# Three instead of two seven-product pairs in the gate/up stage of a two-layer trunk, with its chunks written out as straight code

## The reference

```python
def swiglu_ffn(x, norm_g, w_gate, w_up, w_down):
    h = rms_norm(x, norm_g)
    return (jax.nn.silu(h @ w_gate) * (h @ w_up)) @ w_down
```

## Time and profile before

| | |
|---|---|
| median of 3 runs | 2124.43 us (2124.36 to 2124.97) |
| the profiled execution | 2123.94 us |
| its span | 2121.8 us |
| TensorE busy | 2110.1 us, 99% |
| VectorE busy | 1415.5 us, 67% |
| ScalarE busy | 1079.8 us, 51% |
| DMA queue of the loads | 56.5% of the 16 engines' span |
| HBM | 189 GB/s over the span |

### The profile page before, as it was taken

How to read it: one execution, slowest core, us unless ns; L and a number is a source line. 1 busy time by engine, 2 the same in 40 slices (tenths; PEclk the granted TensorE clock), 3 DMA queues, 4 the chain that set the end, 5 groups by cost and what they waited for, 6 DMA issues and landing times.

```text
span 2121.8 us, 25577 instructions
## 1 busy us (share of the span) xinstructions
PE 2110.1 (99%) x9638; PEld 1751.7 (83%) x9638; DVE 1415.5 (67%) x1553; ACT 1079.8 (51%) x1308; POOL 35.7 (2%) x47
## 2 busy tenths in 40 slices
PE   9999999999999999999999999999999999999999
PEld 7888878888888888888888888878888888888887
DVE  5466577775677578855556565577874677578754
ACT  6443555553444345545566565465553444355532
POOL 1000000000000000000000001000000000000000
PEclk9999999999999999999999999999999999999999
DMA  8655546555655556655555444546555655566653
GB/s 326 209 177 169 175 164 229 178 198 189 213 194 178 198 187 207 201 177 180 197 179 171 165 162 162 172 159 224 171 198 198 215 182 178 198 198 199 210 171 134
DMA packets 202625, 402.80 MB, mean 190 GB/s; under 512 B 7120, under 2 KB 7728, under 8 KB 202288
## 3 DMA queue, kind: packets, MB, share of 16 engines
q1 hardware_dynamic: 201760, 398.49, 56.5%
q0 software_dynamic: 784, 3.19, 0.4%
HBM read 399.56 MB, written 2.10 MB: 189 GB/s over the span
## 4 chain that ended last, share of the span: by engine, by line
PE 97%; DVE 2%; ACT 1%; DMA 0%; issue 0%; SPq 0%; ACTq 0%
PE acc L1252 17%; PE acc L1256 17%; PE acc L1254 17%; PE acc L1393 13%; PE acc L1395 13%; PE acc L1394 13%; PE tr L1300 2%; PE tr L1394 1%; PE tr L1393 1%; PE tr L1395 1%; DVE w_lo L830 0%; DMA raw<-in_a_w_in_dram 0%; DVE a_lo L856 0%; PE tr L1363 0%; PE tr L1515 0%; PE tr L1525 0%
## 5 line engine op out<-in xcount | busy, mean ns | idle before, releaser
L830 DVE TENSOR_TENSOR w_lo<-raw,w_hi 128x1024 fp32r<-128x1024 f32 x567 | 685.0, 1222 | 441.3 <-ACT w_hi L476 440.7
L476 ACT ACTIVATE w_hi<-raw 128x1024 fp32r<-128x1024 f32 x567 | 597.4, 1060 | 674.5 <-PE acc L1256 359.3
L1393 PE MATMUL acc<-w_hi,a_hi 128*128 128x512 f32 x1056 | 412.7, 391 | 3.4 <-DVE w_lo L830 3.4
L1395 PE MATMUL acc<-w_hi,a_lo 128*128 128x512 f32 x1056 | 411.1, 389 | 0.0
L1394 PE MATMUL acc<-w_lo,a_hi 128*128 128x512 f32 x1056 | 410.8, 389 | 0.0
L1252 PE MATMUL acc<-w_hi,h_hi 128*128 128x512 f32 x696 | 271.6, 390 | 0.0
L1256 PE MATMUL acc<-w_hi,h_lo 128*128 128x512 f32 x696 | 270.9, 389 | 0.0
L1254 PE MATMUL acc<-w_lo,h_hi 128*128 128x512 f32 x696 | 270.8, 389 | 0.0
L1252 PE MATMUL acc<-w_hi,a_hi 128*128 128x512 f32 x640 | 255.1, 399 | 0.8 <-DVE a_lo L856 0.5
L1256 PE MATMUL acc<-w_hi,a_lo 128*128 128x512 f32 x640 | 249.8, 390 | 0.0
L1254 PE MATMUL acc<-w_lo,a_hi 128*128 128x512 f32 x640 | 249.4, 390 | 0.0
(11 more groups left out here) (187 smaller groups left out, 2262.6 us busy)
## 6 DMA issues: line engine op xcount, KB each, us to landing
raw<-in_ffn_w_down_dram SPq DMA_DIRECT2D x88, 1024.0 KB, 5.1
raw<-in_ffn_w_gate_dram SPq DMA_DIRECT2D x66, 1024.0 KB, 5.1
raw<-in_ffn_w_up_dram SPq DMA_DIRECT2D x66, 1024.0 KB, 5.1
raw<-in_a_w_in_dram SPq DMA_DIRECT2D x30, 1024.0 KB, 5.5
raw<-in_ffn_w_gate_dram SPq DMA_DIRECT2D x44, 512.0 KB, 3.7
raw<-in_ffn_w_up_dram SPq DMA_DIRECT2D x44, 512.0 KB, 4.5
raw<-in_a_w_out_dram SPq DMA_DIRECT2D x16, 1024.0 KB, 5.1
raw<-in_w_v_dram SPq DMA_DIRECT2D x16, 1024.0 KB, 5.1
```

What stands on the lines that cost most here:

```text
L476: nc.scalar.activation(dst, src, ACT.Copy).then_inc(hi_split, 1)
L830: nc.vector.tensor_tensor(lo, src, hi, ALU.subtract).then_inc(lo_split, 1)
L1393: nc.tensor.matmul(bank[:, :], hi, rhs_hi, start=start, stop=False)
L1395: return nc.tensor.matmul(bank[:, :], lo, rhs_hi, start=False, stop=stop)
```

## The change

WINO becomes 3: half groups 0, 1 and 2 of gate and up are pairs. That holds for the 20 chunks that are not the first of a layer. The first chunk of a layer keeps two pairs and its order. The other chunks have ten half groups and three pairs, in this order (g is gate, u is up, s a pair): g3 g4 g5 g6 g7 u7 s0 u3 s1 u4 s2 u5 u6. The half group u7 now stands ahead of the first pair; between the pairs lies one half group each. The loads follow in an order of their own, with one load of half a gate and half an up pair of half groups (g7 u7). The forms cover three pairs, f_hi and f_lo grow by half, and the sums of the forms are in a buffer of their own, form_a. On VectorE, `pair_sums` of a pair stands after the half group that comes before the pair's own, or, for the pair 0 of a layer's first chunk, after u2 rather than after u3. The transposes of the chunk before move from behind the third half group to behind the second. The wait for `hidden_lo` moves from before pair 0 to before the products in pair 0 that write the banks tr. The loops over chunks become straight code on all engines, the half groups' slot in the ring goes by the running number, and the two semaphores of landed pairs are one for each slot. The work of a chunk's hooks is the same.

The diff, cut to its core (the loads, the down stage, the ScalarE side and the code that works out slots and counts follow the lists in the same way; the code removed on VectorE and SyncE is that of the functions above):

```diff
-    WINO = 2
-    PLAIN = 2 * (KB // HG - WINO)
...
+    WINO = 3
...
+    ORDER_1 = items("g2 g3 g4 g5 u2 u3 g6 s0 g7 u4 u5 s1 u6 u7")
+    LOADS_1 = [items(w) for w in ("g2 g3", "g4 g5", "u2 u3", "g6 g7", "s0", "u4 u5", "s1", "u6 u7")]
+    ORDER_N = items("g3 g4 g5 g6 g7 u7 s0 u3 s1 u4 s2 u5 u6")
+    LOADS_N = [items(w) for w in ("g3 g4", "g5 g6", "g7 u7", "s0", "u3 u4", "s1", "s2", "u5 u6")]
...
-    GU_ORDER = [(m, j) for m in range(2) for j in range(6)]
-    GU_WINO = {5: 0, 9: 1}
-    GU_RAW = (0, 1, 2, 0, 1, 3)
-    GU_WINO_RAW = (3, 2)
-    GU_ORDER_1 = [(0, 0), (0, 1), (0, 2), (0, 3), (1, 0), (1, 1), (0, 4), (0, 5), (1, 2), (1, 3), (1, 4), (1, 5)]
-    GU_WINO_1 = {6: 0, 9: 1}
-    GU_RAW_1 = (0, 1, 2, 3, 1, 3)
-    GU_WINO_RAW_1 = (0, 2)
...
+            form_a = sb("form_a", [P, WINO, CH], F32, part)
...
+            def slot_free(layer, n):
+                what, count = SLOT_READ[layer][n - RAW]
+                sp.wait_ge(s_split if what == "pair" else lo_split, count)
...
+            def forms(layer):
+                a = form_a
+                if layer:
+                    dve.wait_ge(s_used, 3 * (LAST_PAIR[layer - 1, NF - 1] + 1))
+                step.inc(nc.vector.tensor_tensor(a[:, :, :].rearrange("p a c -> p (a c)"),
                                                  a_hi[:, 0:2 * WINO, :].rearrange("p k s -> p (k s)").bitcast(F32),
                                                  a_lo[:, 0:2 * WINO, :].rearrange("p k s -> p (k s)").bitcast(F32), ALU.add))
-                a11, a21, a12, a22 = (sums_b[:, 0:2, n * P:(n + 1) * P] for n in range(4))
-                s1, s2, s3, s4 = (sums_b[:, 2:4, n * P:(n + 1) * P] for n in range(4))
+                a11, a21, a12, a22 = (a[:, :, n * P:(n + 1) * P] for n in range(4))
+                s1, s2, s3, s4 = (sums_b[:, 0:WINO, n * P:(n + 1) * P] for n in range(4))
...
+                        if c == 0:
+                            hooks = {("g", 2): [lambda: forms(layer)], ("g", 4): [lambda: forms_lo_part(layer)],
+                                     ("g", 5): [first_hooks[0][0]], ("u", 2): [lambda: sums(c, 0)],
+                                     ("u", 3): [first_hooks[0][1]], ("u", 4): [lambda: sums(c, 1)]}
+                        else:
+                            hooks = {("g", 6): [], ("u", 7): [lambda: sums(c, 0)], ("u", 3): [lambda: sums(c, 1)],
+                                     ("u", 4): [lambda: sums(c, 2)]}
+                            if c > c0:
+                                hooks[("g", 4)] = [lambda: gate_sums(c - 1)]
+                                hooks[("g", 5)] = [lambda: hidden(c - 1, CHUNK_END[layer, c - 1])]
+                                hooks[("g", 6)].insert(0, lambda: dve.wait_ge(staged, b0 + c - NC))
+                                hooks[("s", 0)] = [lambda: hidden_lo(c - 1, c0)]
+                            else:
+                                hooks[("g", 6)].insert(0, first_hooks[p][0])
...
+                if tr_read is not None:
+                    pe.wait_ge(lhs_lo, tr_read)
                 products(tr[0], form(s1), *t1, start=first, stop=last)
                 products(tr[1], form(s3), *t3, start=first, stop=last).then_inc(s_used, 1)
...
-                        for q, (matrix, j) in enumerate(order):
-                            if first_layer and (matrix, j) == (1, 0):
+                            pe.wait_ge(gate_ready, NF * layer + c)
+                        begun = set()
+                        for item in order(c):
+                            m, q = item
+                            if c == 0 and item == ("u", 2):
                                 pe.wait_ge(staged, b0 - NC)
-                            if first_layer and (matrix, j) == (0, 4):
+                            if c == 0 and item == ("g", 6):
                                 pe.wait_ge(lhs_lo, b0)
-                            begins = j == 0 and (matrix == 0 or first_layer)
-                            plain_group(hg + q, q, matrix, j, (begins, j == 0),
-                                        (matrix == 1 and j == 5, matrix == 1 and j == 5))
-                            if first_layer and q == 3:
+                            if item == ("s", 0) and c == 0:
+                                pe.wait_ge(forms_lo, layer + 1)
+                            if item == ("u", 7) and c:
+                                if c == c0:
+                                    pe.wait_ge(part_added, added)
+                                else:
+                                    pe.wait_ge(staged, b0 + c - NC)
+                            if m == "s":
+                                pair(PAIR_OF[layer, c, q], q, q == 0, q == pairs(c)[-1], "u" not in begun,
+                                     b0 + c if q == 0 else None)
+                                begun |= {"up 0"}
+                            else:
+                                s = "gu".index(m)
+                                if m == "u":
+                                    starts = "u" not in begun and "up 0" not in begun, "u" not in begun
+                                else:
+                                    starts = ("g" not in begun,) * 2
+                                plain_group(HG_OF[layer, c, item], q, s, starts, item == order(c)[-1])
+                                begun |= {m}
+                            if item == ("g", 5) and c == 0:
                                 transpose_batch(b0 - 1)
-                            if not first and q == 2:
-                                transpose_batch(i + (b0 + c0 - 1))
-                            if q in wino:
-                                k = wino[q]
-                                if k == 0:
-                                    if first_layer:
-                                        pe.wait_ge(forms_lo, layer + 1)
-                                    elif first:
-                                        pe.wait_ge(part_added, added)
-                                    else:
-                                        pe.wait_ge(staged, i + (b0 + c0 - NC))
-                                        pe.wait_ge(lhs_lo, i + (b0 + c0))
-                                pair(i * WINO + (WINO * (NF * layer + c0) + k), k, k == 0 and not first_layer)
-                    chunk(0, True, p == 0)
-                    with pe.Fori(1, c1 - c0) as i:
-                        chunk(i, False)
+                            if item == ("g", 4) and c > c0:
+                                transpose_batch(b0 + c - 1)
```

More of the change, by code:

```diff
@@ L350, in down @@
[L350 to L365, removed]
@@ new lines, in down @@
+            def down(layer, p, n):
+                c0, c1 = PARTS[p]
+                for g in range(NC * (c1 - c0)):
+                    c = g // (c1 - c0)
+                    k = 4 * (c0 + g % (c1 - c0))
+                    slot_free(layer, n)
+                    slot = n % RAW
+                    sp.dma_start(raw[:, slot, :, :], w_down_k[layer][:, k:k + 4, c * CH:(c + 1) * CH])\
+                        .then_inc(raw_landed[slot], 16)
+                    n += 1
+                return n
@@ L372, in _ @@
+            def feed_forward(layer):
+                n = RAW
+                for p, (c0, c1) in enumerate(PARTS):
+                    for c in range(c0, c1):
+                        n = gate_up(layer, c, n)
+                    n = down(layer, p, n)
             feed_forward(0)
@@ L693, in feed_forward @@
                     n = 2 * (c1 - c0)
+                    first = LOAD_OF[layer, c1 - 1, loads(c1 - 1)[-1][-1]] + 1
                     for c in range(NC):
-                        counts = [16 * (slot_n[g % RAW] + g // RAW + 1) for g in range(c * n // 2, (c + 1) * n // 2)]
                         if c == 0:
                             hooks = {1: [lambda: read_p1(c1 - 1)], 2: [lambda: silu(c1 - 1)],
-                                     n - 3: [lambda: hidden_hi(c1 - c0 - 1)]}
+                                     n - 3: [lambda: hidden_hi(c1 - 1, c0)]}
@@ L703, in feed_forward @@
                             hooks = {}
-                        unit(hg_before[f"down{layer}{p}"] + n * c, counts, hooks, j0=c * n, n=n)
-                    advance(c1 - c0)
+                        for j in range(n):
+                            slot, count = in_slot(first + (c * n + j) // 2)
+                            plain_hi(DOWN_HG[layer, p] + c * n + j, slot, j % 2, raw_landed[slot], before + count)
+                            for work in hooks.get(j, ()):
+                                work()
+                advance(LAYER_LOADS // RAW)
             feed_forward(0, 1, lambda: save_chunk(1, NC - 1, batches["x1"] + NC - 1),
@@ L1098, in feed_forward @@
                     n = 2 * (c1 - c0)
-                    down = f"down{layer}{p}"
+                    base = DOWN_HG[layer, p]
+                    first = LOAD_OF[layer, c1 - 1, loads(c1 - 1)[-1][-1]] + 1
                     last = p == len(PARTS) - 1
@@ L1420, in form @@
```

(7 more changed lines are left out.)

349 lines of the change are left out of this document (163 added, 186 removed).

## The result

| | before | after |
|---|---|---|
| median | 2124.43 us (2124.09 to 2124.97, 5 runs) | 2134.78 us (2134.51 to 2134.90, 5 runs) |
| the profiled execution | 2123.94 us | 2134.51 us |
| its span | 2121.8 us | 2132.4 us |

A forecast was written before the change was run, and what follows sets the result against it. TensorE, busy 99% of the span, was taken as the bound. Fewer matmuls -13.6, stops +23.2 and layer starts +0.2 gave +9.8 us: 2133.7 for the profiled execution, median 2134.2 us, range 2124 to 2140.

The forecast's parts named there:

- The gain: TensorE in the 20 chunks with a third pair: 3 matmuls less each, 0.68 us a chunk, 13.6 us in all.
- The turnaround: Between pairs, cast and subtractions take 7.93 us against 7.48 of matmuls: TensorE stops 0.45 us, then 0.45 + 0.08.
- the hops: Engine handoffs before a pair: VectorE starts 0.03 us after the cast, TensorE 0.14 after the subtraction; named the first doubt.
- The restart: After each stop, TensorE's next matmul comes 0.08 us late; with the stops, a chunk pays 1.14, rounded to 1.16.
- What was costed at nothing: In the chunks, moved transposes, loads, later casts and straight code cost 0; VectorE is free 0.1 to 0.3 us early.
- The layer starts: First pair of each layer, with larger forms and earlier sums: 1.8 us gained in layer 0, 2.0 lost in layer 1.
- The sum: Whole kernel: -13.6 + 23.2 + 0.2 = +9.8 us, for a median of 2134.2 us.
- Turnaround fits: Rival: between pairs the chain closes inside 7.48 us, only the gain stands, 2111 us; decides at 0.34 a stop; chance 0.10.
- VectorE is the bound: Rival: in the chunks VectorE's serial work adds some 0.5 us to each stop, 20 more, 2154 us; chance 0.05.
- The clock: Rival: TensorE's stops might pull the granted clock down; given nothing of its own, with no chance stated.

The follow-up runs named there:

- Partial waits: Changed kernel, but TensorE waits for a pair's operands in three steps (before its first, fourth and sixth product) instead of once for all seven: 2109.14 us.
- remedied pairs: Two kernels, with two and with three pairs, both with operand waits in three steps and a first chunk's last residual sum ahead of the forms: 2117.40 and 2104.17 us.
- late-sums experiment: Changed kernel, but in a layer's first chunk the sums of pair 0 go back behind u3, as in the kernel before: 2136.67 us.
- the run with two pairs: Changed kernel with its straight code, load lists and hook places, but two pairs in each chunk, in the order of the kernel before: 2121.59 us.
- four pairs: Changed kernel with operand waits in three steps, and four pairs and eight half groups in the 20 chunks, pairs 2 and 3 side by side: 2121.55 us.
- the wider order: Changed kernel with two half groups instead of one between neighbouring pairs, still one wait for all seven operands: 2111.06 us.
- partial waits and the wider order together: Changed kernel with operand waits in three steps and two half groups between neighbouring pairs: 2108.56 us.

## Why the prediction was right

**The gain, 13.6 us.** It can't be seen in the changed kernel by itself. Partial waits show it in the chunk (43.09 to 42.4), two against three remedied pairs in the whole (13.2 by medians, 13.6 by the chunks). By the Trainium skill's figure (TensorE: Matmul & The Clock Gate, section Back-to-back issue gap) it would be 12.9 us, an estimate from 216 ns a matmul. The medians alone can't decide between the two; in the timeline the starts stay 0.2267 apart, not 0.216.

**The turnaround.** The two intervals were forecast as 7.93 and 7.93 + 0.16 us, and are 7.93 and 8.09. Inside, two links were off and cancelled: the cast begins 2.33 us after its pair (2.24 forecast; 2.48 against 2.40 for the second), and TensorE starts 0.05 after the subtraction it waits for (356.37 + 1.22 to 357.64), not 0.14. That the sum is exact to the hundredth is luck. The 2.24 was the row of one chunk; in the kernel before, the same step took 2.24 in 16 chunks and 2.32 in the first chunk of each part but the layers' own, four in all. The 0.14 came from the start of a layer, and there it still holds (the subtraction at 307.90 ends 309.12, TensorE starts 309.26). The doubt that the prediction raised about the hops was in place: had only one of them been off, 40 stops would have made 2 to 4 us of it.

**The restart.** Forecast 0.08, measured 0.11, and some hundredths more on the next matmuls (357.98 to 358.22 is 0.24). The second stop of a chunk is for that reason 0.43 and not 0.53: TensorE itself is later by then, as much as the chain is. In the sum it comes to the same. A chunk was to pay 1.16 us; it pays 0.48 + 0.68 = 1.16. The prediction's terms add up to 1.14, and its rounding to 1.16 had no row behind it; that it fits is luck, worth 0.4 us over 20 chunks.

**What was costed at nothing.** VectorE was to be free 0.1 to 0.3 us before the second cast ends; it idles 0.34 there and its releaser is ScalarE. The cast waits for TensorE's third product, 42 long waits, as said. No wait of TensorE's sequencer appears with straight code.

**The layer starts.** -1.8 and +2.0 forecast, -1.83 and +1.97 measured. The late-sums experiment confirms the step behind the first (+1.9 when undone), and the run with two pairs the cost of the forms: they delay the first half group by 2.0 us in both layers, and in layer 0 the idle time takes up 1.3 of it, as the prediction's chain had it.

**The sum.** From the end of the mixer the changed kernel falls back 3.5 us in layer 0, 0.3 in the attention and 7.0 in layer 1, and it had started 0.4 ahead: 10.4 in all. By the prediction's terms it is 10 x 0.48 - 1.8 = 3.0 and 10 x 0.48 + 2.0 = 6.8. The one long stop is 0.3 of the 0.5 us left in layer 0. The rest, the attention's 0.3 and the 0.2 of layer 1, has no step; it is inside the range.

**The rivals.** "Turnaround fits" would have decided below 0.34 us a stop; a stop costs 0.58 with its restart. "VectorE is the bound" comes near only with four pairs, and there together with the turnaround. The clock was given nothing of its own, which held for stops of 0.45 us but was dismissed too lightly: in layer 1 TensorE stood 2 us for u2, and then:

```profile
1418.88 0.56 PE L1392 MATMUL acc<-w_hi,a_hi 128*128 128x512 f32 x1 [1.99 <-DVE w_lo L1017]
...
1419.23 0.63 PE L1393 MATMUL acc<-w_lo,a_hi 128*128 128x512 f32 x1
...
1419.66 0.63 PE L1394 MATMUL acc<-w_hi,a_lo 128*128 128x512 f32 x1
```

The granted clock is 0.50 from 1419.20 to 1422.40. That lost nothing here, since pair 0 waited for VectorE all the same (1428.52 to 1429.31 above). With no half group between the pairs the same effect cost 27 us.

## What to carry to other kernels

Before packing work that shares one buffer closer together, add up the buffer's turnaround (last reader, cast, subtractions, restart) and compare it with the work that lies between: here 7.93 against 7.48 us turned a gain of 13.6 into a loss of 10. Where it is short by a little, first ask what the waiting instruction really reads: splitting one wait into three, with no other change, was worth 25.6 us, 23.5 of it in the chunks. And rank such stops from start to start, not by the view of waits, which showed 12.9 us for stops that cost 23.

## What the runs showed of the hardware

**The clock can fall after a single long stop.** After the 40 stops of 0.43 to 0.72 us, and after the 20 of 0.9 to 1.06 with four pairs, the granted clock stays at 2.4 GHz. After stops of 3.16 us it fell to 1.2 GHz in 17 of 20 cases, for some eight matmuls; the fall came anywhere from 0.14 us before the restart to 1.52 us after it. After a stop of 2 us at the start of layer 1 it is not certain. It fell in three of the seven profiles that have one: in the changed kernel, with partial waits and with late sums. It did not with the wider order, without a half group between the pairs, with four pairs, and with partial waits and the wider order together. There the matmul at 1405.65 followed the same wait, 1.98 us, and the next came 0.30 later, at full clock:

```profile
1405.65 0.47 PE L1394 MATMUL acc<-w_hi,a_hi 128*128 128x512 f32 x1 [1.98 <-DVE w_lo L1017]
1405.95 0.40 PE L1395 MATMUL acc<-w_lo,a_hi 128*128 128x512 f32 x1
1406.19 0.39 PE L1396 MATMUL acc<-w_hi,a_lo 128*128 128x512 f32 x1
```

Where the fall lies on the path, it makes a 3 us stop cost half as much again.

**A restart isn't one number.** In the steady chunks TensorE starts 0.05 us after the releasing subtraction's end, and its next matmul is 0.11 late, whether it stood 0.45, 0.72 or 3.16 us. At the two layer starts, where the program has another wait of TensorE's ahead of the pair's, the two are 0.14 and 0.08, after 1.12 us as after 0.56. That the second wait is the reason was not tested.
